# Expert products in plain fp32 on column tiles of TensorE, without weight splits, and another order at the seams of the projection pairs

## What is computed

```python
def expert_choice_ffn(h, w_r, b_r, w_g, w_u, w_d):
    n = xt.shape[0]
    cap = EC_FACTOR * n // N_EXPERTS            # 64 for the sample, 16 for the prompt tokens
    aff = jax.nn.softmax(logits, axis=-1)
    gate, idx = lax.top_k(aff.T, cap)
    xe = xt[idx]
    hid = jax.nn.silu(jnp.einsum('ecd,edf->ecf', xe, w_g)) * jnp.einsum('ecd,edf->ecf', xe, w_u)
    ye = jnp.einsum('ecf,efd->ecd', hid, w_d) * gate[..., None].astype(xe.dtype)
    out = jnp.zeros_like(xt).at[idx.reshape(-1)].add(ye.reshape(-1, D_MODEL))
```

## Time and profile before

| | before |
|---|---|
| median of 3 runs | 3142.98 us (3142.4 to 3145.7) |
| profiled execution | 3139.37 us, span of the trace 3137.8 us |
| PE matmul busy | 2971.7 us (95%) |
| VectorE busy | 2160.0 us (69%) |
| ScalarE busy | 1418.6 us (45%) |
| mean granted TensorE clock | 0.982 |
| DMA | 756.74 MB, 241 GB/s over the span |

### The profile page before, as it was taken

The page is one execution under the profiler, slowest core; times in us unless marked ns, Lnnn a source line. Parts: engine busy times, 40 slices in busy tenths (PEclk is TensorE's granted clock), DMA queues, the critical chain, the costliest instruction groups (busy, mean ns, idle before and its releaser), DMA issues.

```text
span 3137.8 us, 50680 instructions
## 1 busy us (share of the span) xinstructions
PE 2971.7 (95%) x20058; PEld 2506.4 (80%) x20058; DVE 2160.0 (69%) x2392; ACT 1418.6 (45%) x1629; POOL 287.9 (9%) x448
## 2 busy tenths in 40 slices
PE   5999999979999999989999998799999999999995
PEld 4899999969999999989999997466666666666664
DVE  5777776556666666664244334899989999999895
ACT  3322233333233333333121222577777777777775
POOL 0011110001111111010011111000000000000000
PEclk9999999989999999999999998899999999999997
DMA  9544432454545454443345334899999999999994
GB/s 400 224 137 127 131 123 94 160 191 168 204 165 191 166 204 177 173 177 126 114 175 170 131 122 169 313 382 380 375 377 385 385 388 388 379 380 374 380 391 149
DMA packets 135493, 756.74 MB, mean 241 GB/s; under 512 B 17616, under 2 KB 32000, under 8 KB 60880
## 3 DMA queue, kind: packets, MB, share of 16 engines
q1 hardware_dynamic: 102992, 636.54, 53.1%
q0 software_dynamic: 32336, 117.83, 12.1%
HBM read 686.84 MB, written 60.91 MB: 238 GB/s over the span
## 4 chain that ended last, share of the span: by engine, by line
PE 74%; DVE 11%; DMA 6%; issue 5%; ACT 3%; POOL 0%; SPq 0%; DVEq 0%; ACTq 0%; POOLq 0%
PE pu L1106 24%; PE pu L741 10%; PE pu L742 10%; PE pu L743 10%; DVE elo L2217 4%; PE pt L720 2%; PE pt L923 2%; DMA raw<-in_w_ada 2%; ACT ehi L1483 2%; DMA blocks<-in_w_in 2%; PE pu L823 2%; PE pu L826 2%; PE pu L825 2%; PE ps L823 1%; PE ps L826 1%
## 5 line engine op out<-in xcount | busy, mean ns | idle before, releaser
L2217 DVE TENSOR_TENSOR elo<-ering,ehi 128x2048 fp32r<-128x2048 f32 x384 | 874.7, 2288 | 108.7 <-ACT ehi L1483 104.2
L1483 ACT CAST ehi<-ering 128x2048 fp32r<-128x2048 f32 x384 | 731.4, 1912 | 239.5 <-PE pu L1106 239.3
L741 PE MATMUL pu<-hhi,whi 128*128 128x320 f32 x2144 | 680.2, 317 | 14.3 <-DVE hlo L1987 9.1
L743 PE MATMUL pu<-hhi,wlo 128*128 128x320 f32 x2144 | 664.2, 310 | 0.0
L742 PE MATMUL pu<-hlo,whi 128*128 128x320 f32 x2144 | 663.9, 310 | 0.0
L741 PEld LDWEIGHTS pu<-hhi,whi 128*128 128x128 f32 x2144 | 404.4, 189 | 23.0 <-issue 15.8
L742 PEld LDWEIGHTS pu<-hlo,whi 128*128 128x128 f32 x2144 | 404.5, 189 | 1.6
L743 PEld LDWEIGHTS pu<-hhi,wlo 128*128 128x128 f32 x2144 | 404.0, 188 | 0.0
L1106 PE MATMUL pu<-ehi,xhi 128*80 128x512 f32 x1024 | 322.1, 396 | 2.1
L1106 PE MATMUL pu<-ehi,xlo 128*80 128x512 f32 x1024 | 320.8, 395 | 0.0
L1106 PE MATMUL pu<-elo,xhi 128*80 128x512 f32 x1024 | 320.0, 394 | 0.0
(11 more groups left out here) (368 smaller groups left out, 4494.4 us busy)
## 6 DMA issues: line engine op xcount, KB each, us to landing
ering<-in_w_experts SPq DMA_DIRECT2D x384, 1024.0 KB, 8.0
raw<-in_w_ada SPq DMA_DIRECT2D x96, 1024.0 KB, 8.2
blocks<-in_w_in SPq DMA_DIRECT2D x72, 512.0 KB, 4.3
raw<-in_w_in SPq DMA_DIRECT2D x34, 1024.0 KB, 5.0
...
```

What stands on the lines that cost most here:

```text
L741: nc.tensor.matmul(o, whi[:, dk, w:w + 128], hi[:, kt, cols], start=kt == 0, stop=False)
L743: last = nc.tensor.matmul(o, wlo[:, dk, w:w + 128], hi[:, kt, cols], start=False, stop=kt == kts - 1)
L1483: nc.scalar.copy(ehi[:, j % AHEAD, :], ering[:, slot, :]).then_inc(ex_hi, 1)
L2217: nc.vector.tensor_tensor(elo[:, j % AHEAD, :], ering[:, slot, :], ehi[:, j % AHEAD, :].bitcast(F32), ALU.subtract).then_inc(ex_lo, 1)
```

## The change

**Experts.** The unit is no longer split. TensorE reads `ering` itself, in plain fp32, against a plain fp32 stationary operand (`xt`, `ht`). The 64 sample slots and the 16 prompt slots (padded with zeros to 32) are separate stationary operands: the sample product of a k-tile has its 1024 columns cut in two parts of 512 on two 64-column tiles, the prompt product in four parts of 256 on four 32-column tiles. The slot of the ring is free when TensorE has read it. ScalarE copies transposes and does the two silus, VectorE the gating, the modulation and the outputs. The outputs lie on 128 partitions in column parts, so each expert is added into HBM by four indirect DMAs of 128 rows instead of one of 80; the padded slots go to 16 extra rows of `tokens_acc`. New indices and gates for this (`idup`, `vdup`, then `idx2`, `gate2`) are formed after the top-k.

**Seams of the pairs.** `sums_next` of the next pair comes right after `sums_first`, ahead of `combine(v, 3)`, and `fast_lo` of the next pair's first product stands inside it.

**Opening of the attention.** `conv_rows` and the first taps move from k = 0 to k = 1, and SP's wait before the fourth load of the stage is for an earlier product (the fourth of the last pair's seven, not the last).

```diff
+    xt, o = at("xt", [128, KT, WIDE], F32, o)
+    ht, o = at("ht", [128, 2, 384], F32, o)
...
-    ehi, o = at("ehi", [128, AHEAD, UNIT], F32R, o)
-    elo, o = at("elo", [128, AHEAD, UNIT], F32R, o)
...
@@ -446,7 +449,7 @@
                 for b in range(2):
                     at_ = G_S + 3 * k + 1 + b
                     if i == 0 and k == 0 and b == 1:
-                        sp.wait_ge(st_mm, MM_ALL)
+                        sp.wait_ge(st_mm, product(FAST - 1, 3) + 1)
                     load(a["w_ada"][i * (2 * US) + (A1 + 2 * k + b)], at_ % RAW, at_ // RAW + i * (3 * US // RAW))
         for name, first, n in (("w_attn_out", G_T, TN), ("w_conv_out", G_C, CN), ("w_out", G_O, ON)):
...
+            row = rows_d[16 * s:16 * s + 16, :].rearrange("a c -> (a c)")
+            pool.dma_start(shslot[p0:p1, :], row.partition_broadcast(p1 - p0)).then_inc(slots_loaded, 16)
+        for s, dst, n, wide in ((0, g2l, 2, 64), (1, g2c, 4, 32)):
+            for t in range(n):
+                for h in range(2):
...
-        def scatter(e):
-            pool.indirect_dma_start(acc_d[:, :], bass.IndirectOffsetOnAxis(ap=idx_all[:, e:e + 1], axis=0), ysl[:, :],
-                                    None, compute_op=ALU.add).then_inc(y_added, 16)
+        def scatter(e, h, signal):
+            for dst, c, src in ((acc_l, 0, yl), (acc_c, 1, yc)):
+                pool.indirect_dma_start(dst[:, :], bass.IndirectOffsetOnAxis(ap=idx2[:, c, e:e + 1], axis=0), src[:, h, :],
+                                        None, element_offset=1024 * h, compute_op=ALU.add).then_inc(signal, 16)
 
...
             if e + 1 < NE:
-                pool.wait_ge(y_made, 2 * e + 4)
-                scatter(e)
+                for h in range(2):
+                    pool.wait_ge(y_made, 2 * e + 3 + h)
+                    scatter(e, h, y_added)
         for h in range(2):
             pool.wait_ge(y_made, 2 * NE + 1 + h)
-            pool.indirect_dma_start(acc_d[:, :], bass.IndirectOffsetOnAxis(ap=idx_all[:, NE - 1:NE], axis=0),
-                                    ysl[:, 1024 * h:1024 * h + 1024], None, element_offset=1024 * h,
-                                    compute_op=ALU.add).then_inc(y_last[h], 16)
+            scatter(NE - 1, h, y_last[h])
         pool.wait_ge(vx_stored, 16 * NKV)
         pool.wait_ge(rope_stored, 16 * (2 * NKV + NH))
...
                     pe.wait_ge(y_made, 2 * e + (j // 8 + 1))
                 if j in (0, 2, 4, 6):
-                    pe.wait_ge(psu_lo, TURNS * e + (3 + j // 2))
+                    pe.wait_ge(psu_copied, TURNS * e + (3 + j // 2))
                 if j in (16, 18):
-                    pe.wait_ge(psu_lo, TURNS * e + (7 + (j - 16) // 2))
-                pe.wait_ge(ex_lo, e * EU + (j + 1))
+                    pe.wait_ge(psu_copied, TURNS * e + (7 + (j - 16) // 2))
+                slot = (j + LEAD) % ERING
+                pe.wait_ge(slot_loaded[slot], 32 * e + (16 * (j // ERING + 1) + used_slot(slot)))
                 h = j // 8 if j < 16 else 2 + (j - 16) // 4
                 kts = KT if h < 2 else FT
-                for b in range(2):
-                    k = 2 * (j % 8 if h < 2 else j % 4) + b
-                    hi, lo = (xhi[:, k, :], xlo[:, k, :]) if h < 2 else (hthi[:, k, :], htlo[:, k, :])
-                    for left, ring in ((hi, ehi), (hi, elo), (lo, ehi)):
-                        for c in range(2):
-                            w = 1024 * b + 512 * c
-                            last = nc.tensor.matmul(pu[0:SLOTS, 2 * (h % 2) + c, :], left, ring[:, j % AHEAD, w:w + 512],
-                                                    start=k == 0 and left is hi and ring is ehi,
-                                                    stop=k == kts - 1 and left is lo)
+                for c, parts, wide in ((0, 2, 512), (1, 4, 256)):
+                    for b in range(2):
+                        k = 2 * (j % 8 if h < 2 else j % 4) + b
+                        q = k % 4
+                        if h < 2:
+                            left = xt[:, k, CAPL:WIDE] if c else xt[:, k, 0:CAPL]
+                        elif c:
+                            left = ht[:, k // 4, 256 + 32 * q:288 + 32 * q]
+                        else:
+                            left = ht[:, k // 4, 128 * (q % 2) + 64 * (q // 2):128 * (q % 2) + 64 * (q // 2) + 64]
+                        for t in range(parts):
+                            g, w, half = 128 // parts, 1024 * b + wide * t, wide // 2
+                            moving = ering[:, slot, w:w + wide]
+                            if h < 2:
+                                moving = ering[:, slot, 1024 * b:1024 * b + 1024].rearrange("p (s f) -> p s f", s=2)[
+                                    :, :, half * t:half * t + half]
+                            last = nc.tensor.matmul(pu[g * t:g * t + g, 2 * c + h % 2, 0:wide], left, moving, start=k == 0, stop=k == kts - 1,
+                                                    skip_group_check=True)
                 last.then_inc(ex_mm, 1)
                 if j == 9:
...
-                if following and 18 <= j < 22:
-                    g = j - 18
-                    turned_hi(xhi[:, 4 * g:4 * g + 4, :], TURNS * e + (6 + g), g % 2)
+            for h in range(2):
+                silu(e, h)
+                hid_copy(h, TURNS * e + 4 + h, h)
+            if following:
+                for g in range(4):
+                    slots_copy(g, TURNS * e + 6 + g, g % 2)
 
         def tile_root(g):
             act.wait_ge(fin_c, 5 * FAST + 7 * g + 3)
...
@@ -1730,7 +1745,9 @@
 
             a11, a21 = place(v, 0), place(v, 2)
             vec.wait_ge(s_made, 4 * v + 1)
+            vec.wait_ge(blk_loaded[a11], 16 * (PLAIN + v + 1))
             nc.vector.tensor_tensor(blk[a21], blk[a11], blk[a21], ALU.subtract).then_inc(s_made, 1)
+            fast_lo(v, 0)
             vec.wait_ge(s_made, 4 * v + 2)
...
@@ -1854,13 +1870,11 @@
             fast_lo(v, 6)
             if v + 1 < FAST:
                 sums_first(v + 1)
+                sums_next(v + 1)
             else:
                 vec.wait_ge(glu_z, CT - 1)
                 vec.sem_inc(psum_free[0], SKIP // 2)
             combine(v, 3, c2b[:, 0:HALF], b_, e1[:, :], 5)
-            if v + 1 < FAST:
-                fast_lo(v + 1, 0)
-                sums_next(v + 1)
             if turns:
                 turn_end(NKV + 2 * before + 1)
         vec.wait_ge(st_mm, product(FAST - 1, 3) + 1)
...
@@ -1954,11 +1968,6 @@
                     if i == 0 and k == 0:
                         if x == 0:
                             split_lo(*raw_use(G_S, 3, US, 0, 1), QN + GN + 1, 1)
-                        elif x == 1:
-                            conv_rows()
-                            conv(i, k, 0, parts)
-                        else:
-                            conv(i, k, 1, parts)
                     if x == 0 and k:
                         next_unit(k - 1)
                     if k == US - 1 and i + 1 < SN // US:
@@ -1966,7 +1975,14 @@
                         conv(i, k, 0, 2)
                         normalise(i + 1, 0)
                         conv(i, k, 1, 2)
-                    elif i or k or x == parts - 1:
+                    elif i == 0 and k == 1:
+                        if x == 0:
+                            conv_rows()
+                        if x < 2:
+                            conv(i, 0, x, 2)
+                        else:
+                            conv(i, 1, 0, 1)
+                    elif i or k:
                         conv(i, k, x, parts)
             first = i * (2 * US) + A1
             add_bias(i + (KT + 1), slice(first, first + 2 * US) if isinstance(i, int) else ds(first, 2 * US), pt[:, 1, :],
...
         assert rv[0] == RV_END, (rv, RV_END)
-        vec.sem_inc(psu_lo, 2)
         vec.sem_inc(y_made, 2)
-
-        def unit_lo(e, j):
-
-            vec.wait_ge(ex_hi, e * EU + (j + 1))
-            slot = (j + LEAD) % ERING
...
+                last = nc.vector.scalar_tensor_tensor(out=dst, in0=up, scalar=gate, in1=dst, op0=ALU.mult, op1=ALU.mult)
+            last.then_inc(hid_done, 1)
 
         def slots_y(e, h):
 
             vec.wait_ge(ex_mm, e * EU + (20 + 4 * h))
             if h == 0:
                 vec.wait_ge(y_free, e + 1)
-            cols = slice(1024 * h, 1024 * h + 1024)
-            nc.vector.tensor_tensor(ysl[:, cols].rearrange(c2, c=2), pu[0:SLOTS, 2 * h:2 * h + 2, :],
-                                    g2slot[:, cols].rearrange(c2, c=2), ALU.mult).then_inc(y_made, 1)
-
-        vec.wait_ge(slots_loaded, 64)
-        for j in range(2):
-            unit_lo(0, j)
+            nc.vector.tensor_tensor(yl[:, h, :], pu[:, h, :], g2l[:, h, :], ALU.mult)
+            nc.vector.tensor_tensor(yc[:, h, :], pu[:, 2 + h, 0:256], g2c[:, h, :], ALU.mult).then_inc(y_made, 1)
+
+        vec.wait_ge(slots_loaded, 16 * 14)
+        for b in range(2):
+            vec.wait_ge(acc_stored[b], 16 * (ON // 2))
...
```

(23 more changed lines are left out.)

143 lines of the change are left out of this document (71 added, 72 removed).

## The result

The changed kernel takes **3160.2 us** (median of 4 runs, 3159.3 to 3160.7) against 3142.7 us before (4 runs, 3139.4 to 3145.7), a ratio of 1.0054 with a 95% interval of 1.0039 to 1.0069: slower, by 17.5 us, where 18 had been forecast. The profiled execution's span is 3159.1 us, against 3137.8 us, 21.3 us more. In all that follows, the executions compared ran at a mean granted clock of 0.97 to 0.99; one execution of `e12` at 0.84 (3364.5 us) is left out of its ratio.

What follows compares the result with a forecast made beforehand. TensorE, busy 95% of the span, was taken to set the pace, with DMA close behind. Terms -16 - 4 + 35 + 8 - 7 - 1 + 3 = +18 us on the 3143.0 us median gave 3161 us; 8-in-10 range 3075 to 3188.

Steps and rivals of the forecast that it cites:

- The experts, +35 us: Expert units on TensorE: streaming falls to 2.60 us, two switches add 0.26 us, so 0.09 us more over 384 units.
- a rival at 0.22: Expert units: no drain between 64 and 32 columns, a unit takes 2.60 us, total 3061 to 3099 us; chance 0.22.
- the rule that would expose every group's load: Expert units: weight loads overlap matmuls only where row groups differ; would add 104 us, left out as contradicted by the trace.
- Turns +8 us: Six groups of transposes an expert: each pays a switch of its own, 0.08 us for each of 96.
- hidden activations -7 us: Expert stage: TensorE's waits for hidden activations go, as ScalarE's casts and VectorE's `elo` leave the queues.
- Opening, -16 us: Opening of the attention: waits of 16.2 and 3.3 us and 1.5 us of lost clock go, less a 5 us charge.
- The charge of 5 us: Opening of the attention: cost of the rest of the convolution rows' landing and of 8 taps in one piece.
- Seams, -4 us: Seams of the pairs: 0.4 us less waiting for `blo` at each of some ten seams.
- Start -1 us: Start of the experts: VectorE's four `xlo` leave the path to the first unit; the gather hides the new small operations.
- end +3 us: Adds into HBM: at the end each half has two indirect DMAs in series ahead of the final norm's loads.
- DMA's share, below 0.97: Expert stage, a sign in the trace after: DMA's busy share should fall below 0.97.
- The loop's code: Expert loop's jump back waits for code: 15 jumps at up to 7 us, up to +105 us, 3161 to 3266; chance 0.05.

Runs made afterwards that it cites:

- e12: e6 with a branch hint at the head of TensorE's expert loop that announces the jump back: 3120.0 us (0.9920).
- e4: Changed kernel with the order of 64-column and 32-column products alternating from unit to unit, one switch a unit instead of two: 3120.3 us (0.9934).
- e5: Changed kernel with sample and prompt products alternating for each half of the columns, four switches a unit instead of two: 3269.6 us (1.0400).
- e7: Changed kernel with each 64-column product split into two of 32 columns with the same moving columns, no switch, 384 calls: 3073.5 us (0.9775).
- e11: e7 with the convolution taps of the first attention unit handed out two at a time: 3066.3 us (0.9754).
- e3: Kernel before the change, with only the changed order of VectorE's work at the seams of the block products: 3141.4 us (0.9991).
- e6: Changed kernel with all expert products on 32-column tiles, 576 product calls an expert instead of 288 and six adds instead of four: 3171.6 us (1.0101).

## Why the prediction was right, point by point

**The experts, +35 us: right for the reason given.** The unit came out at 2.87 us (forecast 2.86), 0.10 us more than before or 38 us over 384 units: 2.58 of streaming (2.60) and 0.29 of switches (0.26). That 64 to 32 columns drains was an inference from rows with 128 columns on one side, with a rival at 0.22. `e4`, `e5` and `e7` settle it with one, four and no switches. The groups of four stand 0.216 us apart with new weights each time, so the rule that would expose every group's load stays contradicted, as in the forecast.

**Turns +8 us and hidden activations -7 us: half right.** The hidden activations came as forecast, the turns' term was mis-sized. By the distances of first products, what an expert takes beyond its units went from 2.76 us (69.26 - 24 x 2.771) to 2.64 (71.50 - 24 x 2.869), -2 us over the stage where +1 was forecast. The waits for the hidden activations went, 6.9 us. The turns cost at most some 5 us and not 8, because they stand at a border that pays a switch anyway. The forecast charged the switch twice.

**Opening, -16 us: the mechanism right, a term of the sum mis-sized.** The stretch from the first attention product to the last turn shrank by 10.7 us, 5 less than forecast. The long stop and the 3.3 us for `pt_sb` went, as forecast. The charge of 5 us for what comes late next was 9.6 us in the trace. Of it 5.3 us are the taps, by the timeline of DVE (`maxima` of the next step stands behind them):

```profile
656.29 2.82 DVE L1941 SCALAR_TENSOR_TENSOR ctmp<-zt,taps,ctmp 128x670 f32<-128x670 f32 x3
...
668.00 7.59 DVE L1941 SCALAR_TENSOR_TENSOR ctmp<-zt,taps,ctmp 128x670 f32<-128x670 f32 x8
```

as `e11` confirms, where they are gone. Another 2.4 us is a wait that the forecast did not have:

```profile
648.42 0.27 ACT L1375 COPY ao<-pt 128x128 f32<-128x128 f32 x1 [5.49 <-DMA att<-ao]
```

ScalarE's copy of a head's output waits for the store of an earlier one, and the exponentials queue behind it. Before, the long stop covered that: no wait for this store stands in the trace before. The last 1.5 us, two waits of 0.85 and 0.63 us, were not followed up.

**Seams, -4 us: not contradicted in size,** 3 us by fourteen executions, 0 to 6 by `e3`, 0.5 us in the changed kernel's own trace; a single trace could not have told it from nothing. The total of `blo` waits fell by a tenth, not by a third as the forecast said. They moved from the second product of the pair to the first.

**Start -1 us and end +3 us: within the scatter.** From the last turn of the attention to the first `xe` transposes it was 661.0 us before and 658.4 after, but anything from 657.5 to 662.5 in the twelve experiments. The gather did hide the new operations on VectorE whole, as forecast: the last of them ends at 1964.28, and VectorE then still waits for the gather.

```profile
1964.09 0.19 DVE L2276 CAST idx<-pt 128x32 uint32<-128x32 f32 x1
1966.04 2.73 DVE L2231 SCALAR_TENSOR_TENSOR xe<-xe,shslot 80x512 f32<-80x512 f32 x4 [1.76 <-DMA xe<-tokens_z,idx_all]
```

TensorE's two waits here, 3.9 us for `idup` and 3.1 for `xe`, are together less than the 9.4 us for `xe` before. After the last product the kernel takes 45 us as before; the second add in each half did not show. The +3 us stood on 2.3 us of POOL an add, scaled by rows; one took 1.54 us.

**DMA's share, below 0.97: wrong.** It stayed at 1.00. The forecast took the share for utilisation. It stood at 1.00 at 376 GB/s without a wait for the ring and at 1.02 at 398 GB/s with one, so only the wait tells the bound.

**The loop's code, a rival with 0.05:** right to price it low for this body, and the runs show that it was one factor of two away. (The rival counts 15 jumps; 15 turns have 14, as the gaps of `e6` show.) The Trainium skill, Runtime: NRT & Kernel Launch, Instruction fetch mechanics, puts the limit at 2048 instructions. Counted in records of products and loads (four a call, its transposes not counted), a body of 384 calls has 1536 and shows no gap, one of 576 has 2304 and shows it. That brackets the Trainium skill's figure and agrees with it.

The total was right within 1 us of 18, and that is luck. Against the difference of the two profiled executions, 21.3 us, the terms were off by +5 (opening), +3 (units), +3.5 (seams, in this execution), -3 (turns and waits), -4 (end) and -2 us (start), and all but 3 us of it cancelled. What deserved trust was the sign.
